# The first modulation in four column groups of TensorE, x loaded first, and latent columns moved by 16

## What is computed

```
def reference(x, c, ctx, c_ctx, w_ada, b_ada, ...):
    s_lat = jax.nn.silu(c)                 # (1, 1024)
    s_ctx = jax.nn.silu(c_ctx)[None]       # (1, 1024)
    for l in range(DEPTH):
        mod = s_lat @ w_ada[l] + b_ada[l]      # 9 * 1024 outputs
        mod_c = s_ctx @ w_ada[l] + b_ada[l]
        x, xc = trunk_layer(x, xc, mod, mod_c, p, ctx_out=l < DEPTH - 1)
    return rmsnorm(x, norm_final)

def ffn_sublayer(s, m, g_norm, w_in, w_out):
    h = rmsnorm(s, g_norm) * (1.0 + m[1]) + m[0]
    return s + 0.5 * m[2] * swiglu(h, w_in, w_out)
```

## Time and profile before

| | us |
|---|---|
| median of 3 runs (2257.09 to 2266.88) | 2259.07 |
| the profiled execution | 2265.39 |
| its span | 2263.7 |
| TensorE matmuls busy | 2159.6 (95%) |
| VectorE busy | 1359.9 (60%) |
| ScalarE busy | 882.0 (39%) |
| first product of `ffn(0)` starts at | 52.70 |

### The profile page before, as it was taken

How to read it: one execution, slowest core, us unless ns; L and a number is a source line. 1 busy time by engine, 2 the same in 40 slices (tenths; PEclk the granted TensorE clock), 3 DMA queues, 4 the chain that set the end, 5 groups by cost and what they waited for, 6 DMA issues and landing times.

```text
span 2263.7 us, 33728 instructions
## 1 busy us (share of the span) xinstructions
PE 2159.6 (95%) x12654; PEld 1837.2 (81%) x12654; DVE 1359.9 (60%) x2277; ACT 882.0 (39%) x1375; POOL 219.5 (10%) x287
## 2 busy tenths in 40 slices
PE   6999999999999999999999999999999988798998
PEld 3788878988677777988888888888899767788998
DVE  5778877543556547498874265555365654665554
ACT  3433322534553334432222253332244553345543
POOL 0001023000011100310011100001110001001001
PEclk8999999999999999999999999999999999899999
DMA  6455554423111224365554344444343320154555
GB/s 266 153 198 186 197 166 150 138 84 94 56 52 61 71 81 166 112 204 197 192 181 114 105 139 139 148 143 129 99 130 126 98 72 27 58 184 145 181 173 151
DMA packets 96912, 303.86 MB, mean 134 GB/s; under 512 B 10672, under 2 KB 17328, under 8 KB 95920
## 3 DMA queue, kind: packets, MB, share of 16 engines
q1 hardware_dynamic: 77520, 232.96, 31.6%
q0 software_dynamic: 18720, 69.21, 9.1%
q10 hardware_dynamic: 576, 0.34, 0.0%
HBM read 291.99 MB, written 10.49 MB: 134 GB/s over the span
## 4 chain that ended last, share of the span: by engine, by line
PE 54%; DVE 5%; ACT 3%; DMA 1%; issue 1%; DVEq 0%; ACTq 0%; SPq 0%
PE ps L2042 16%; PE ps L2043 16%; PE ps L2044 16%; DVE w_lo L1454 1%; ACT w_hi L825 1%; PE ps L2408 1%; PE ps L2411 1%; PE ps L2419 1%; PE ps L2230 0%; PE ps L2358 0%; PE ps L2480 0%; PE ps L2478 0%; DMA raw<-in_w_down 0%; PE ps L2432 0%; PE ps L2310 0%
## 5 line engine op out<-in xcount | busy, mean ns | idle before, releaser
L2042 PE MATMUL ps<-h_hi,w_hi 128*128 128x512 f32 (+1 forms) x2176 | 774.8, 356 | 29.0 <-DVE w_lo L1454 11.7
L1454 DVE TENSOR_TENSOR w_lo<-raw,w_hi 128x1024 fp32r<-128x1024 f32 (+2 forms) x416 | 475.7, 1147 | 474.7 <-ACT w_hi L825 470.8
L2043 PE MATMUL ps<-h_lo,w_hi 128*128 128x512 f32 (+1 forms) x2176 | 758.1, 348 | 0.0
L2044 PE MATMUL ps<-h_hi,w_lo 128*128 128x512 f32 (+1 forms) x2176 | 758.0, 348 | 0.0
L825 ACT ACTIVATE w_hi<-raw 128x1024 fp32r<-128x1024 f32 (+2 forms) x416 | 404.3, 974 | 616.0 <-DMA raw<-in_w_down 309.2
L2042 PEld LDWEIGHTS ps<-h_hi,w_hi 128*128 128x128 f32 x2176 | 416.0, 191 | 107.6 <-issue 31.3
L2044 PEld LDWEIGHTS ps<-h_hi,w_lo 128*128 128x128 f32 x2176 | 416.1, 191 | 51.7
L2043 PEld LDWEIGHTS ps<-h_lo,w_hi 128*128 128x128 f32 x2176 | 416.5, 191 | 48.7
L2042 PE MATMUL ps<-a_hi,w_hi 128*128 128x512 f32 (+1 forms) x1050 | 359.8, 343 | 11.3 <-DVE w_lo L1454 4.2
L2043 PE MATMUL ps<-a_lo,w_hi 128*128 128x512 f32 (+1 forms) x1050 | 357.1, 340 | 0.0
L2044 PE MATMUL ps<-a_hi,w_lo 128*128 128x512 f32 (+1 forms) x1050 | 357.1, 340 | 0.0
(11 more groups left out here) (259 smaller groups left out, 1752.6 us busy)
## 6 DMA issues: line engine op xcount, KB each, us to landing
raw<-in_w_up SPq DMA_DIRECT2D x176, 512.0 KB, 3.8
ada<-in_w_ada_t POOLq DMA_DIRECT2D x128, 512.0 KB, 3.9
raw<-in_w_down SPq DMA_DIRECT2D x64, 384.0 KB, 3.2
raw<-in_w_gate SPq DMA_DIRECT2D x48, 512.0 KB, 3.5
raw<-in_w_down SPq DMA_DIRECT2D x64, 320.0 KB, 2.9
raw<-in_w_proj SPq DMA_DIRECT2D x32, 512.0 KB, 3.4
raw<-in_w_merge SPq DMA_DIRECT2D x16, 512.0 KB, 3.6
raw<-in_w_out SPq DMA_DIRECT2D x16, 512.0 KB, 3.3
```

Of the source, the lines that this page charges most:

```text
L1454: vec.tensor_tensor(w_lo[:, j % RING, 0:cols], raw[:, j, 0:cols], w_hi[:, j % RING, 0:cols].bitcast(F32), ALU.subtract).then_inc(s_lo, 1)
L2042: pe.matmul(out, wh, rows_hi[:, i, c], start=first, stop=False)
L2043: pe.matmul(out, wh, rows_lo[:, i, c], start=False, stop=False)
L2044: return pe.matmul(out, wl, rows_hi[:, i, c], start=False, stop=last)
```

## The change

All 2048 outputs of the first modulation are now made by TensorE. Each of its 8 input tiles is one slice of 128x2048 of `w_ada`, and makes four matmuls of 512 columns, whose outputs go to the partitions 0, 32, 64 and 96 of one PSUM bank: the stationary `c_act` is widened from 2 to 32 columns (30 are zero, by a memset on GpSimd). One copy of 128x512 and four turns of 128x128 bring them back. VectorE's 16 instructions are gone. `x` is the first load; the weights follow in five loads. GpSimd issues `c_wide` and `ada` only when the last of them has landed. The sums of squares use a 128x128 block of ones as the stationary operand, so that the sums stand on all partitions at once: 8 matmuls of 512 columns in place of 32 of one column, the root and the reciprocal are taken of 128x512, and the spread (L2014) is gone. The activation of `c_wide` moves behind `norm(0)`. ScalarE's copy of `ada_rows` comes ahead of its first two casts, and VectorE's first two lowers come behind its first two multiplications. Where only latent tokens are left, `h_hi`, `h_lo`, `a_hi` and `a_lo` hold them in columns 16 to 271 instead of 0 to 255; no product changes its size. Addresses from `x` on are as before.

```
+ROW_GROUP = 32
+FIRST_PARTS = ((0, 2), (2, 2), (4, 2), (6, 1), (7, 1))
+LATE = 16
...
-            ada_first = sb("ada_first", [P, ADA_FIRST, KD * P], at=s)
-            ada_rows = sb("ada_rows", [P, 2, TOK], at=s)
+            ada_first = sb("ada_first", [P, KD, ADA_FIRST * P], at=s)
+            ada_rows = sb("ada_rows", [P, TOK], at=s)
+            c_act = sb("c_act", [P, KD, ROW_GROUP], at=s)
...
+        mod_first = ps[:, 3, :].rearrange("p (c g j) -> p g c j", c=KD // 2, j=ROW_GROUP)[:, :, :, 0:2]
...
+        def ffn_cols(f):
+            return slice(LATE, LATE + LAT) if n_tok(f) == LAT else slice(0, TOK)
+        def norm_cols(s):
+            return ffn_cols(FFN_STAGE.index(s))
+        def merge_cols(l):
+            return slice(LATE, LATE + LAT) if l else slice(0, TOK)
...
         def _(sp):
             sp.dma_start(x[:, :, :], a["xT"]).then_inc(s_x, 16)
-            for m in range(2):
-                for i in (3, 1):
-                    load_first(i, i * q + m * q // 2, q // 2, late=3 * m)
+            for i, (k, n) in enumerate(FIRST_PARTS):
+                sp.dma_start(ada_first[:, k:k + n, :], a["w_ada"][k:k + n].rearrange("k p n -> p k n")).then_inc(s_first[i], 16)
...
         def _(pool):
+            pool.memset(c_act[:, :, :], 0.0).then_inc(s_set, 1)
...
+            pool.wait_ge(s_first[len(FIRST_PARTS) - 1], 16)
             load_c(0)
             load_ada(0, wait=False)
...
-            act.activation(c_act[:, :, :], c_in[:, :, :], ACT.Silu).then_inc(s_cact, 1)
-            act.wait_ge(s_set, 3)
+            act.wait_ge(s_set, 4)
+            act.activation(c_act[:, :, 0:2], c_in[:, :, :], ACT.Silu).then_inc(s_cact, 1)
-            wide(0)
...
-                act.activation(rms[:, 0:n // P], ps[:, 6, 0:n // P], ACT.Sqrt, bias=eps_col[:, 0:1],
+                act.activation(rms[:, 0:root_width(s, n)], ps[:, 6, 0:root_width(s, n)], ACT.Sqrt, bias=eps_col[:, 0:1],
                                scale=1.0 / D).then_inc(s_rt, 1)
                 if s == 0:
+                    act.wait_ge(s_adad, 1)
+                    act.activation(ada_rows[:, :], ps[:, 2, :], ACT.Copy).then_inc(s_adr, 1)
                     casts(0, 2)
-                    act.wait_ge(s_adad, 1)
-                    act.activation(ada_rows[0:2, :, :], ps[0:2, 2:4, :], ACT.Copy).then_inc(s_adr, 1)
...
-                    act.activation(h_hi[:, k, 0:n], buf_b[:, k % 2, 0:n], ACT.Copy).then_inc(s_hhi, 1)
+                    act.activation(h_hi[:, k, norm_cols(s)], buf_b[:, k % 2, 0:n], ACT.Copy).then_inc(s_hhi, 1)
...
             norm(0, 0, 0, TOK)
+            wide(0)
             ffn(0)
...
-                if s < 6:
+                if 0 < s < 6:
                     lowers(0, 2)
                 if s:
                     inverse_root(s, n)
+                    vec.wait_ge(s_bc, part(s))
+                    spread = ps[:, 6, 0:n]
                 else:
                     modulations(0, 0, 2)
+                    vec.wait_ge(s_inv, 1)
+                    spread = inv[:, 0:n]
...
                 scaled(0)
                 for k in range(KD):
                     if k + 1 < KD:
                         scaled(k + 1)
+                    if s == 0 and k == 0:
+                        lowers(0, 2)
...
-                    vec.tensor_tensor_reduce(ps[:, 4:6, :].rearrange("p b n -> p (b n)"), ada_first[:, KD + t, :],
-                                             c_wide[:, i, :], 1.0, 0.0, ALU.mult, ALU.add,
-                                             scale_first[:, t, i:i + 1]).then_inc(s_adv, 1)
+            inverse_root(0, TOK)
...
                 for k in range(KD):
                     pe.wait_ge(s_fsq, k + 1)
-                    for t in range(TT):
-                        ins = pe.matmul(ps[:, 6, t:t + 1], first_sq[:, k, t * P:(t + 1) * P], ones[:, 0:1],
-                                        start=k == 0 and t == 0, stop=k == KD - 1, skip_group_check=True)
+                    ins = pe.matmul(ps[:, 6, :], ones[:, :], first_sq[:, k, :], start=k == 0, stop=k == KD - 1)
...
+            def first_mods():
+                pe.wait_ge(s_cact, 1)
+                for i, (k0, n) in enumerate(FIRST_PARTS):
+                    pe.wait_ge(s_first[i], 16)
+                    for k in range(k0, k0 + n):
+                        for g in range(4):
+                            rows = slice(g * ROW_GROUP, (g + 1) * ROW_GROUP)
+                            ins = pe.matmul(ps[rows, 2, :], c_act[:, k, :], ada_first[:, k, g * TOK:(g + 1) * TOK],
+                                            start=(k == 0), stop=(k == KD - 1))
...
+            def turn_mods():
+                pe.wait_ge(s_adr, 1)
+                for c in range(KD // 2):
+                    cols = slice(c * P, (c + 1) * P)
+                    ins = pe.transpose(ps[:, 3, cols], ada_rows[:, cols], ident)
```

More of the change, by code:

```diff
@@ L151, in build_program @@
         c_in = sb("c_in", [P, KD, 2])
-        c_act = sb("c_act", [P, KD, 2])
         ada_sum = sb("ada_sum", [P, 4])
-        scale_first = sb("scale_first", [P, KD, 2])
-        sb("pad_rows", [P, 8])
+        sb("pad_rows", [P, 40])
         x = sb("x", [P, KD, TOK])
@@ L345, in build_program @@
         s_gain = sem("final_gain_loaded")
-        s_first = [sem(f"ada_first_loaded{i}") for i in range(7)]
+        s_first = [sem(f"ada_first_loaded{i}") for i in range(5)]
         s_raw = [sem(f"raw_loaded{i}") for i in range(RING)]
@@ L722, in load_ada @@
                         pool.wait_ge(s_adu, 4 * r + 2 * j - 2)
-                    pool.dma_start(ada[:, j, :], a["w_ada_t"][ADA_FIRST - KD + 2 * r + j]).then_inc(s_ada[j], 16)
+                    pool.dma_start(ada[:, j, :], a["w_ada_t"][2 * r + j]).then_inc(s_ada[j], 16)
             def mixer_pool(l):
@@ L943, in upper @@
                         act.wait_ge(s_mul, p0 + q + 1)
-                        act.activation(a_hi[:, q, 0:n], buf_b[:, j, 0:n], ACT.Copy).then_inc(s_ahi, 1)
+                        act.activation(a_hi[:, q, ffn_cols(f)], buf_b[:, j, 0:n], ACT.Copy).then_inc(s_ahi, 1)
                     return silu, upper
@@ L1062, in y_upper @@
                     k = Y_ORDER[j]
-                    act.activation(a_hi[:, KD + k, 0:no], y[:, k, 0:no], ACT.Copy).then_inc(yhi.sem, 1)
+                    act.activation(a_hi[:, KD + k, merge_cols(l)], y[:, k, 0:no], ACT.Copy).then_inc(yhi.sem, 1)
                 for n in range(N_PROJ + 3):
@@ L1266, in mixer_act @@
                     act.wait_ge(mg.sem, mg.at(l, i + 1))
-                    act.activation(a_hi[:, i, 0:no], buf_b[:, 0, 0:no], ACT.Copy).then_inc(mhi.sem, 1)
+                    act.activation(a_hi[:, i, merge_cols(l)], buf_b[:, 0, 0:no], ACT.Copy).then_inc(mhi.sem, 1)
                 for i in range(KD + 3, 2 * KD):
@@ L1329, in inverse_root @@
                 vec.wait_ge(s_rt, part(s) + 1)
-                vec.reciprocal(inv[:, 0:n // P], rms[:, 0:n // P]).then_inc(s_inv, 1)
+                vec.reciprocal(inv[:, 0:root_width(s, n)], rms[:, 0:root_width(s, n)]).then_inc(s_inv, 1)
             def norm(s, n, final=False):
@@ L1354, in scaled @@
                         vec.wait_ge(s_hhi, KD * part(s) + k - 1)
-                    vec.tensor_tensor(buf_a[:, k % 2, 0:n], x[:, k, 0:n], ps[:, 6, 0:n], ALU.mult).then_inc(s_t, 1)
+                    vec.tensor_tensor(buf_a[:, k % 2, 0:n], x[:, k, 0:n], spread, ALU.mult).then_inc(s_t, 1)
                 scaled(0)
@@ L1404, in scaled @@
                     if k == 0:
-                        vec.wait_ge(s_bc, part(s, p) + 1)
+                        vec.wait_ge(s_bc, part(s, p))
                     if k >= 4:
@@ L2010, in norm @@
                 else:
-                    turn_shifts()
+                    turn_mods()
+                    return
                 pe.wait_ge(s_inv, part(s) + 1)
@@ L2044, in products, with dense @@
                 return pe.matmul(out, wl, rows_hi[:, i, c], start=False, stop=last)
-            def dense(j, b, bank, n, hi=h_hi, lo=h_lo, at=0):
+            def dense(j, b, bank, n, hi=h_hi, lo=h_lo, cols=None):
                 pe.wait_ge(s_lo, b + 1)
                 for k in range(KD):
-                    ins = products(ps[:, bank, 0:n], hi, lo, j, k, at + k, n, k == 0, k == KD - 1)
+                    ins = products(ps[:, bank, 0:n], hi, lo, j, k, k, cols or n, k == 0, k == KD - 1)
                 return ins
@@ L2094, in first_two @@
                     for m in range(2):
-                        ins = products(ps[:, m, 0:n], h_hi, h_lo, m, k, k, n, k == 0, k == KD - 1)
+                        ins = products(ps[:, m, 0:n], h_hi, h_lo, m, k, k, norm_cols(s), k == 0, k == KD - 1)
                         if k == KD - 1:
@@ L2127, in down @@
                         for k in range(k0, k1):
-                            ins = products(ps[:, 4 + j, 0:n], a_hi, a_lo, m, k - k0, k, n, k == 0, k == KF - 1)
+                            ins = products(ps[:, 4 + j, 0:n], a_hi, a_lo, m, k - k0, k, ffn_cols(f), k == 0, k == KF - 1)
```

(2 more changed lines are left out.)

78 lines of the change are left out of this document (22 added, 56 removed).

## The result

| | before | changed |
|---|---|---|
| median of the runs, us | 2264.31 (7 runs, 2257.09 to 2266.88) | 2244.51 (7 runs, 2238.95 to 2253.25) |
| ratio, 95% interval | | 0.9921 (0.9904 to 0.9938) |
| the profiled execution, and its span | 2265.39, 2263.7 | 2238.95, 2237.3 |
| TensorE matmuls busy | 2159.6 (95%) | 2136.5 (95%) |
| VectorE busy | 1359.9 | 1342.5 |

The changed kernel is faster by 19.8 us between the medians, 0.8%; the forecast was 2244.4. The median of before is 5.2 us above the one that the forecast started from, so the agreement in the total is closer than the agreement in the gain: 14.7 us were forecast. That the 5.1 us missing in the gain and the 5.2 us in the starting point cancel is luck. The profile shows which terms were met and which was not.

The account below looks back on a forecast made before the run. The prediction took TensorE's queue at the start as the bound, with `x` late and 64 small passes in it. A gain of 15.5 less 0.8 for the lowers gave 14.7 us, hence 2244.4 us, range 2226 to 2252.

Parts of the forecast that it names:

- The bound and the loads: At the start, TensorE's queue bounds; with `c_wide` and `ada` waiting, the last weights land at 28.9 us, otherwise 5 us later.
- The sums: Sums of squares at the start: 16 passes, 4.4 of them at the slow pace, take 8.8 us and end at 18.3.
- The reciprocal: VectorE's reciprocal of 128x512 at the start: 4.3 us at most, costed at nothing under the weights' landing.
- Four groups: Modulation matmuls on TensorE run four at a time, 0.85 us for a tile of four groups.
- The clock: Last modulation tile and turns run at 1.2 GHz, first shift at 34.6; at 2.4 GHz 33.0, or 33.6 behind the casts.
- The two lowers: VectorE's lowers, moved behind its first two multiplications, end 2.8 us after the first shift: a price of 0.8 us.
- Moved at no price: Activation of `c_wide` moved into `ffn(0)`, GpSimd's held loads and the memset cost nothing; an early load would make it 1.4 us.
- The latent columns: 1968 products in `ffn(3)` and the second merge start at column 16: effect taken as 0, bounds 24.6 us either way.
- rival 1: Moved latent columns speed up products: half the fixed part saves 12.3 us more (2232), all gives 2220; chance 0.27.
- Delivery: Rival at the start: groups two at a time or weights landing 2 us late, gain 10 to 11 us, 2249; chance 0.13.
- the groups did not run one by one: Rival in the modulation: groups run singly, tiles end at 45.8, first shift 49.6 or later, 2259 us; chance 0.05.
- the slower rival: Latent columns starting at 64 bytes cost time per product; with the fixed part doubled 2269 us; chance 0.05.

Follow-up runs that it names:

- Experiment 3: The changed kernel without GpSimd's wait ahead of `c_wide` and `ada`, which load at once: 2254.73 us in one run.
- experiment 2: The changed kernel with the latent tokens back in columns 0 to 255: 2250.41 us, ratio 0.994 to the kernel before.
- experiment 8: The changed kernel with weights shifted 64, 32 or 960 bytes, the last two with latent columns at 0: ratios 1.0058 and 1.008 to before; 2253.38 us.
- experiment 7: The changed kernel with latent columns starting at 8, 32, 64; at 240, 248, 112; or all at 240: 2243.86, 2240.75 and 2243.75 us.
- experiment 6: The changed kernel with the old one-column sums, root and reciprocal of 128x4, and the spread: 2240.83 us in one run.
- experiment 4: The changed kernel with `x` loaded behind the weights: 2257.75 us in one run.

## Why the prediction was right, and where it was not

- **The bound and the loads.** Right. The sums of squares began at 9.87 (9.5 in the sum), the weights landed at 24.5, 26.9 and 29.3 (24, 26.4, 28.9). Experiment 3 confirms the price of `c_wide` and `ada`, 4.9 us for the 5 that the prediction gave.
- **The sums.** 9.73 us from 9.87 to 19.6, for 8.8 from 9.5 to 18.3. The slow pace lasted to 15.1, six passes of 0.85 where 4.4 were taken. It cost nothing, as the weights came later.
- **The reciprocal.** 3.35 us; 4.3 was the upper bound, in proportion to 128x72. It ended at 23.7, and the price of nothing held.
- **Four groups.** They run at once: a tile is over in 0.9 to 1.06 us. Against 0.43 for each of the 32 passes of four tiles, 13.8 us, the 3.64 measured are a factor of 3.8. The Trainium skill's figure in "TensorE: Matmul & The Clock Gate", Part 3, 2.38 for three tiles, is lower than what this trace has for four, and the measurement decides.
- **The clock.** In the profiled execution of the changed kernel this choice failed. The prediction took 1.2 GHz for the last tile and the turns, since TensorE would be idle most of the time. The granted clock stayed at 1.00 until 35.6: the tile took 1.06 for 1.7, the turns 0.63 (and four passes, not eight) for 1.7. The other bound, 2.4 GHz with a shift at 33.6, was the nearer one: the shift came at 33.15, a gain of 16.9 for 15.5. But experiment 2 has the same start and the low clock: 1.62 for the tile, 1.09 for the turns, and the shift at 34.34, inside the forecast 33.6 to 34.6. Of the eight profiled kernels with this start three had the clock at 0.50 from 29.9 to 31.3 on, five only from 34.1 to 36.0 on. The gaps ahead of the tiles do not tell them apart: the longest was 1.74 to 2.59 us in the three and 1.08 to 2.09 in the five. So either bound can come, up to 1.2 us apart, and what decides is open. The casts did not stand ahead of it as feared: `raw` was there, and they ended at 32.94.
- **The two lowers.** Right, 0.9 for a forecast of 0.8. The first `h_lo` starts 2.70 after the first shift (1.8 before), and from the shift to the first product are 3.53 us where the earlier trace rows have 2.62: 0.9. ScalarE's third pair of shifts then waits 0.61 for `buf_a` (the row at 37.17). 16.9 - 0.9 is the 16.0.
- **Moved at no price.** Right for `c_wide`: its activation now stands in `ffn(0)`, and the next cast still waits for its load, 1.38 in place of 2.72. From the timeline of ScalarE:

```profile
50.92 1.92 ACT L829 ACTIVATE c_wide<-c_wide 128x2048 f32<-128x2048 f32 x1
...
54.70 1.06 ACT L833 ACTIVATE w_hi<-raw 128x1024 fp32r<-128x1024 f32 x1 [1.38 <-DMA raw<-in_w_up]
```

- **The latent columns.** Here a term of the sum failed, and it is the step that the prediction had wrong: 0 was taken, "as the pace did not hang on the column in the rows there are". Those rows all had starts on multiples of 1024 bytes, as the prediction itself said, so they were no evidence for 64. It was rival 1 at a sixth of its full size: 2.2 of 12.5 ns. The runs show that the pace of 256 columns lies between 113 and 120 ns, and that of 512 between 227 and 233, when only the distance between the two operands is changed. The Trainium skill ("TensorE: Matmul & The Clock Gate", Part 2) says that "Loading the next tile's weights doesn't steal SBUF read bandwidth from the running matmul", by which the starts would not matter; here they do. That the two reads meet somewhere would fit, but no run looked at it: what inside the chip does it stays open.
- **The sum.** 16.0 + 4.3 = 20.3 for 14.7. The forecast of the time came out nearer than its gain, by luck: it stood on the median of three runs, 2259.07, where seven give 2264.31.
- **The rivals.** Delivery was on time, the groups did not run one by one, and the moved columns did not cost. Of the slower rival the place was right: other shifts, of experiment 8, do make the kernel 0.6 to 0.8% slower.

## What to carry to other kernels

At a kernel's start, the order of loads and the order of the consumer's queue are one decision: put first what the rest waits for, in both, and hold back loads of other queues that share the rate until the last one needed has landed. When a trace shows only one kind of alignment, it says nothing on others; two more starts of an operand cost a line each to try, and are tried for every width of product that they touch. And before a change of a few us is judged by a single run's total, it is worth seeing how far the stages that it leaves alone differ, and how long the granted clock was low in them.

## What the runs showed of the hardware that was not expected

- The pace of a product hangs on the start of its moving operand relative to its stationary one: starts 32 bytes apart already differ, and 256 and 512 columns differ in which start is good (experiments 7 and 8). At a distance of 64 bytes there are two paces for 256 columns, 113.3 and 117.8 ns, and a stretch without a gap mostly keeps the one that it has.
- One execution of the same code differs from another by up to 11 us in the middle 1950 us, mostly with the time that the granted clock stood at 0.50, 50 to 74 us of it.
- After 13.8 us in which TensorE did nothing but one-column matmuls, six rounds ran at half pace, though the granted clock is recorded as 1.00 in that stretch, as it is over the one-column passes (experiment 6). In the kernel before, the same passes averaged 0.62, and the first passes of the earlier trace rows took 0.85 beside a recorded 1.00. So the time from pass to pass tells the pace; the recorded clock alone does not.
- Four column groups of 128x32 with 512 f32 columns each lose almost nothing beside each other: 64 passes in 7.07 us (experiment 4).
- A reciprocal of 128x512 f32 took 3.35 us on VectorE, and one of 128x72 0.60: 6.2 ns for each further column.
